# A mixer and 32 experts on one Trainium2 core: expert 0's first features gathered in quarters on a weight layout of its own, and chunk 7 loaded in four pieces

## What is computed

```
hn  = rmsnorm(x, norm_mix)
z   = gelu(hn @ w_in);  u, v = split(z)            # w_in 2048 x 4096
v   = layernorm(v);     sv = (w_s * causal) v + b_s   # in chunks of 128 tokens, 8 groups
h   = x + (u * sv) @ w_out                          # w_out 2048 x 2048
t   = rmsnorm(h, norm_ffn)
g   = softmax(t @ w_group + b_group); best group;  two best of its 8 experts, with weights
y   = sum over the two experts e of weight * ((silu(t @ w_gate[e]) * (t @ w_up[e])) @ w_down[e])
out = rmsnorm(h + y, norm_final)
```

## Time and profile before

| | |
|---|---|
| median of 3 runs | 1198.08 us (1197.81 to 1198.56) |
| the profiled execution | 1198.11 us, of it 1196.4 us span |
| busy: PE, PEld, DVE, ACT, POOL | 74%, 42%, 32%, 19%, 2% of the span |
| moved by DMA | 460.93 MB, 385 GB/s over the span |
| chain that ended last | DMA 50%, PE 47% |

### The profile page before, as it was taken

One profiled execution on the slowest core, in us unless ns is written; L12 is line 12 of the kernel. 1 busy time (PEld: TensorE's weight loads), 2 busy tenths in 40 slices (PEclk: granted clock), 3 DMA queues, 4 the chain that ended last, 5 costly groups with the idle time before them and its releaser, 6 DMA issues.

```text
span 1196.4 us, 17569 instructions
## 1 busy us (share of the span) xinstructions
PE 883.5 (74%) x7809; PEld 501.8 (42%) x7809; DVE 381.3 (32%) x493; ACT 231.6 (19%) x390; POOL 23.0 (2%) x66
## 2 busy tenths in 40 slices
PE   9999999999984666666666666666666666666666
PEld 7888888877431222222223232222222222222222
DVE  5454866545232222222222222222222222222233
ACT  6644655444200000000000000000000000000003
POOL 1200000000200000000000000000000000000000
PEclk9999999999997777778778787878787887878788
DMA  9875567878999999999999999999999999999997
GB/s 291 327 255 193 193 225 245 302 264 315 399 424 433 429 433 429 434 431 433 433 428 433 434 431 432 434 429 434 431 433 432 430 432 435 429 431 435 426 425 334
DMA packets 47686, 460.93 MB, mean 385 GB/s; under 512 B 4025, under 2 KB 4641, under 8 KB 32289
## 3 DMA queue, kind: packets, MB, share of 16 engines
q1 hardware_dynamic: 46704, 457.19, 92.4%
q0 software_dynamic: 864, 3.21, 0.8%
q10 hardware_dynamic: 80, 0.02, 0.0%
HBM read 458.05 MB, written 2.36 MB: 385 GB/s over the span
## 4 chain that ended last, share of the span: by engine, by line
DMA 50%; PE 47%; SPq 1%; ACT 1%; DVE 1%; issue 1%; POOLq 0%; DVEq 0%
DMA high_slots<-in_e_w_up 48%; PE scattered_out L1395 21%; PE bank L1605 12%; PE bank L1703 5%; PE pair L1566 3%; PE scattered_out L1716 1%; PE pair L1574 1%; DMA out_h<-acc 1%; ACT arena L780 1%; SPq L453 0%; DMA h<-in_x 0%; DVE acc L1261 0%; SPq L469 0%; PE pair L1582 0%; PE bank L1502 0%
## 5 line engine op out<-in xcount | busy, mean ns | idle before, releaser
L1199 DVE TENSOR_TENSOR acc<-scattered_out,acc 128x2048 f32<-128x2048 f32 x58 | 132.9, 2292 | 616.9 <-PE scattered_out L1716 616.9
L1605 PE MATMUL bank<-low_slots,arena 128*32 128x256 f32 x2048 | 153.5, 455 | 147.4 <-DMA low_slots<-in_e_w_up 147.0
L1605 PE MATMUL bank<-high_slots,arena 128*32 128x256 f32 x1952 | 146.0, 457 | 138.4 <-DMA high_slots<-in_e_w_up 138.4
L1605 PEld LDWEIGHTS bank<-low_slots,arena 128*32 128x32 f32 x2048 | 83.9, 126 | 218.8 <-issue 188.8
L1605 PEld LDWEIGHTS bank<-high_slots,arena 128*32 128x32 f32 x1952 | 79.6, 127 | 206.3 <-issue 178.7
L893 DVE TENSOR_TENSOR w_lo<-w_raw,w_hi 128x1024 fp32r<-128x1024 f32 x95 | 116.5, 1226 | 113.8 <-ACT w_hi L601 113.4
L601 ACT CAST w_hi<-w_raw 128x1024 fp32r<-128x1024 f32 x95 | 99.9, 1051 | 126.8 <-PE scattered_out L1395 120.7
L1395 PE MATMUL scattered_out<-w_hi,xT_second 128*128 128x512 f32 x376 | 121.4, 394 | 0.2 <-DVE w_lo L893 0.2
L1395 PE MATMUL scattered_out<-w_hi,xT_first 128*128 128x512 f32 x376 | 120.5, 393 | 0.1
L796 ACT COPY arena<-bank 128x256 f32<-128x256 f32 x32 | 11.9, 372 | 547.9 <-PE bank L1605 547.9
L1703 PE MATMUL bank<-down_slots,arena 128*32 128x512 f32 x944 | 107.9, 596 | 0.7 <-DVE arena L1193 0.7
(11 more groups left out here) (271 smaller groups left out, 512.1 us busy)
## 6 DMA issues: line engine op xcount, KB each, us to landing
down_slots<-in_e_w_down SPq DMA_DIRECT2D x26, 4096.0 KB, 21.1
low_slots<-in_e_w_gate SPq DMA_DIRECT2D x13, 4096.0 KB, 30.2
low_slots<-in_e_w_up SPq DMA_DIRECT2D x13, 4096.0 KB, 39.3
high_slots<-in_e_w_gate SPq DMA_DIRECT2D x13, 4096.0 KB, 30.5
high_slots<-in_e_w_up SPq DMA_DIRECT2D x13, 4096.0 KB, 39.7
w_raw<-in_a_w_in SPq DMA_DIRECT2D x64, 512.0 KB, 3.7
w_raw<-in_a_w_out SPq DMA_DIRECT2D x32, 512.0 KB, 5.0
down_slots<-in_e_w_down SPq DMA_DIRECT2D x6, 2048.0 KB, 19.4
```

Of the source, the lines that this page charges most:

```text
L1199: dve.tensor_tensor(acc[:, t, :], OUT[:, :], (acc if e else h)[:, t, :], ALU.add).then_inc(acc_done, 1)
L1605: ins = pe.matmul(GU[c * CAP:(c + 1) * CAP, 0:256], rows_k, gate_columns(rows_of[c // 2][k], c % 2), start=(a == 0 and k == 0), stop=(a == ...
```

## The change

Four things are changed.

1. Expert 0's gate and up weights (chunks 0 to 3) are loaded in another layout: partition p holds rows p, 128 + p, 256 + p and so on, eight separate rows of 2 KB instead of one piece of 16 KB. A gather for expert 0 now takes 128 neighbouring columns of `h`, and the gains come from `g_ffn`, which stands in that layout already.
2. Of the first eight steps' features, two quarters of 512 features are gathered, copied, transposed and scaled one after the other. The first quarter's four gate steps need only the first. VectorE's product for the first quarter and ScalarE's copy for it stand ahead of the sums and exponentials of the routing weights. The gather of the second half of the features stands behind gate steps 0 to 3 now, whole; before, one token tile of it stood ahead of gate step 0, and the other behind step 1.
3. Chunk 7 is loaded in four parts of 512 KB (rows c and c + 4, after `w_used` 89 + c).
4. The last half of the last block (half 7) goes into raw slot 0 instead of 3, so it waits for `lo_done` 93 instead of 92, and chunk 8's part over raw slot 3 is loaded first, after `lo_done` 92, the one over slot 0 last.

```diff
-        XE_FIRST, TRX_FIRST = GU[:, 256:512], TRX[:, 256:512]
+        XE_FIRST = (GU[:, 256:384], XE[:, 256:384])
+        TRX_FIRST = (TRX[:, 256:384], TRX[:, 384:512])
...
+        def raw_of(n, hc):
+            return 4 if n == 3 * NB - 1 and hc == HC - 1 else hc % 4
...
                 w, a = (e_gate, e_up)[c % 2], c // 2
+                if e == 0:
+                    return w[0, 0].rearrange("(k p) n -> p k n", p=P)[:, 8 * a:8 * a + 8, :]
                 return w[0, e].rearrange("(p a k) n -> a p k n", a=2, k=8)[a]
...
-                    sp.wait_ge(lo_done, HC * n + hc - 3)
-                sp.dma_start(w_raw[:, hc % 4, :, :], src).then_inc(raw_in[hc % 4], 16)
+                    sp.wait_ge(lo_done, HC * n + hc - 3 + raw_of(n, hc) // 4)
+                r = raw_of(n, hc) % 4
+                sp.dma_start(w_raw[:, r, :, :], src).then_inc(raw_in[r], 16)
...
-            sp.wait_ge(w_used, 3 * NB * HC - 6)
-            load_rows(7, 0, x_in[1])
-            sp.wait_ge(w_used, 3 * NB * HC - HC // 2)
-            load_rows(7, 1, chunk_in[chunk_at(7)[0]])
-            for q in range(4):
-                if q == 3:
-                    sp.wait_ge(w_used, 3 * NB * HC - 2)
-                    load_rows(9, 0, x_in[0])
-                sp.wait_ge(lo_done, 3 * NB * HC - 3 + q)
...
+            def load_pair(c, landed):
+                sp.wait_ge(w_used, 3 * NB * HC - 7 + c)
+                sp.dma_start(chunk_tile(7)[:, c:8:4, :], expert_chunk(7)[:, c:8:4, :]).then_inc(landed, 16)
+            def load_raw(q, count, landed):
+                sp.wait_ge(lo_done, count)
+                sp.dma_start(chunk_tile(8)[:, 2 * q:2 * q + 2, :], expert_chunk(8)[:, 2 * q:2 * q + 2, :]).then_inc(landed, 16)
+            load_pair(0, x_in[1])
+            load_pair(1, x_in[2])
+            load_raw(3, 3 * NB * HC - 4, raw_in[3])
+            load_pair(2, x_in[3])
+            load_half(w_out_half((NB - 1) * NBLK, HC - 1), 3 * NB - 1, HC - 1)
+            load_pair(3, chunk_in[chunk_at(7)[0]])
+            load_raw(1, 3 * NB * HC - 2, raw_in[1])
+            load_raw(2, 3 * NB * HC - 1, raw_in[2])
+            sp.wait_ge(w_used, 3 * NB * HC - 2)
+            load_rows(9, 0, x_in[0])
+            load_raw(0, 3 * NB * HC, chunk_in[chunk_at(8)[0]])
...
+            act.wait_ge(xe_first_ps, 1)
+            act.copy(xe[:, 0:P], XE_FIRST[0]).then_inc(xe_first, 1)
             for i in range(2):
                 act.wait_ge(exp_in, i + 1)
                 act.activation((g_exp, e21)[i], (g_shifted, d21)[i], ACT.Exp).then_inc(exp_done, 1)
+            act.wait_ge(xe_first_ps, 2)
+            act.copy(xe[:, P:2 * P], XE_FIRST[1]).then_inc(xe_first, 1)
...
+            dve.wait_ge(exp_in, 2)
+            dve.wait_ge(xeT_first_ps, 1)
+            scale_first(0, 1, TRX_FIRST[0], xeT_first)
             dve.wait_ge(exp_done, 2)
...
             def first_expert():
-                for t in range(NT):
-                    ins = gather_first(0, t)
-                ins.then_inc(xe_first_ps, 1)
+                gather_quarter(0, 0)
+                gather_quarter(0, 1).then_inc(xe_first_ps, 1)
+                gather_quarter(1, 0)
                 pe.wait_ge(xe_first, 1)
-                transpose_first(0).then_inc(xeT_first_ps, 1)
-                gather_first(1, 0)
+                transpose_quarter(0).then_inc(xeT_first_ps, 1)
+                gather_quarter(1, 1).then_inc(xe_first_ps, 1)
...
                 pe.wait_ge(xeT_first, 1)
                 gate_up_of(0, 0, rows_of, 0, 2).then_inc(gu_pair, 1)
-                gather_first(1, 1).then_inc(xe_ps, 1)
+                pe.wait_ge(xe_first, 2)
+                transpose_quarter(1).then_inc(xeT_first_ps, 1)
                 gate_up_of(0, 0, rows_of, 2, 4).then_inc(gu_pair, 1)
+                gather_second_half(0)
+                gather_second_half(1).then_inc(xe_ps, 1)
+                pe.wait_ge(xeT_first, 2)
                 gate_up_of(0, 0, rows_of, 4, 8).then_inc(gu_half, 1)
```

More of the change, by code:

```diff
@@ L393, in _ @@
             for n in range(NB):
-                for hc in range(HC):
+                for hc in range(HC if n < NB - 1 else HC - 1):
                     load_half(w_out_half(n * NBLK, hc), 2 * NB + n, hc)
@@ L599, in hi_half @@
                     act.wait_ge(w_used, HC * n + hc - 1)
-                act.wait_ge(raw_in[hc % 4], 16 * (2 * n + hc // 4 + 1))
-                act.copy(w_hi[:, hc % 2, :, :], w_raw[:, hc % 4, :, :]).then_inc(hi_done, 1)
+                r = raw_of(n, hc) % 4
+                act.wait_ge(raw_in[r], 16 * (2 * n + hc // 4 + 1 + raw_of(n, hc) // 4))
+                act.copy(w_hi[:, hc % 2, :, :], w_raw[:, r, :, :]).then_inc(hi_done, 1)
             def gelu_block(n, parity, dst, done):
@@ L1031, in _ @@
                 for hc in range(HC):
-                    lo_half(n, hc)
+                    lo_half(n, hc, raw_of(n, hc))
                     if hc == 1:
@@ L1175, in _ @@
             g_of = g_rows[:, :].rearrange("p (b k) -> p k b", k=KC).unsqueeze(3).to_broadcast([P, KC, NQ, CAP])
[L1177 to L1184, removed]
             def scale_xeT(e):
@@ L1583, in transpose_scat, with gather_quarter, gather_second_half, transpose_quarter @@
                 ins.then_inc(scat_ps, 1)
-            def gather_first(half, t):
+            def gather_quarter(q, t):
                 pe.wait_ge((sel_first, sel_ready)[t], 1)
                 for j in range(NB):
-                    cols = h[:, t, :].rearrange("q (p a j b) -> q a j p b", a=2, j=NB, b=2)[:, half, j, :, :]
-                    ins = pe.matmul((XE_FIRST, XE)[half][j * CAP:(j + 1) * CAP, 0:2 * P], sel[:, 0, t, :], cols,
+                    col = q * NBLK + j * P
+                    ins = pe.matmul(XE_FIRST[q][j * CAP:(j + 1) * CAP, :], sel[:, 0, t, :], h[:, t, col:col + P],
                                     start=(t == 0), stop=(t == NT - 1))
                 return ins
[L1594 to L1598, removed]
-                return ins
+            def gather_second_half(t):
+                for j in range(NB):
+                    cols = h[:, t, :].rearrange("q (a j p) -> q a j p", a=KC, j=NB)[:, 2:4, j, :]
+                    ins = pe.matmul(XE[j * CAP:(j + 1) * CAP, 0:2 * P].rearrange("c (a p) -> c a p", a=2), sel[:, 0, t, :],
+                                    cols, start=(t == 0), stop=(t == NT - 1))
+                return ins
+            def transpose_quarter(q):
+                return pe.transpose(TRX_FIRST[q], xe[:, q * P:(q + 1) * P], ident[:, :])
             def gate_up_of(e, a, rows_of, lo, hi):
                 for k in range(lo, hi):
-                    rows_k = xeT[:, 2 * a + k % 2, k // 2, :] if e == 0 else xeT[:, k % KC, 2 * a + k // KC, :]
+                    rows_k = xeT[:, 2 * a + k // KC, k % KC, :] if e == 0 else xeT[:, k % KC, 2 * a + k // KC, :]
                     for c in range(NQ):
@@ L1648, in wait_chunk @@
                 if i == 7:
-                    pe.wait_ge(x_in[1], 32)
+                    for c in range(3):
+                        pe.wait_ge(x_in[1 + c], 32)
                 if i == 9:
@@ L1652, in wait_chunk @@
                 if i == 8:
-                    for q in range(3):
-                        pe.wait_ge(raw_in[q], 16 * (3 * NB * HC // 4 + 1))
+                    for q in range(1, 4):
+                        pe.wait_ge(raw_in[q], 16 * (3 * NB * HC // 4 + (1, 1, 0)[q - 1]))
                 if i == 17:
```

24 lines of the change are left out of this document (14 added, 10 removed).

## The result

| | median | lowest to highest | runs |
|---|---|---|---|
| before | 1198.32 us | 1197.15 to 1199.95 | 22 |
| after | 1200.72 us | 1199.33 to 1202.17 | 22 |

The ratio is 1.0020, 95% interval 1.0014 to 1.0025: 2.4 us slower, where 1.2 us of gain was forecast. The profiled execution took 1201.8 us, 1.1 us above the median of its kernel, and its span is 1199.7 us (before 1196.4). So the traces differ by 3.3 us where the medians differ by 2.4.

A forecast was written before the change was run, and what follows sets the result against it. The prediction took TensorE's mixer to bound the kernel up to about 292 us and DMA bytes after; chunk 7, half 7 and the rows at 0 plus 0.70 and 0.50 from two holes gave 1.2 us gain: 1196.9 us, range 1196.0 to 1198.3.

The forecast's parts named there:

- What bounds the kernel: TensorE's mixer up to about 292 us; behind it the end is a sum of DMA bytes, at 431 GB/s from 333 us.
- Chunk 7 in four pieces: Mixer's end, 273 to 293 us: at most 2.5 us of queue time moved forward, all given back by 293; value 0.
- Half 7 later by a step: Last output block: issued at 278.2 instead of 275.44, landing 283.3 to 285.5, hidden until 286.2; cost 0, at most 1.7 us.
- Chunks 0 to 3 in rows of 2 KB: Expert 0's weight loads during the mixer: 0.5 us more for chunk 2, bounds 0 and 2.3, hidden by 1.1 us cover.
- The first features in quarters: Expert 0's first gates, about 298 to 308 us: `gu_pair` 1 earlier by 0.85 us, `gu_pair` 2 by 1.2, `gu_half` by 0.3.
- The sum: DMA holes at 303 to 305 and 306 to 308: 0.70 plus 0.50 gives 1.2 us gain, all reaching the end.
- the dry moment of 292: Queue falls to 229 GB/s in 292 to 294 us, awaiting the mixer's last matmul; only unused DMA time behind it counts.
- the holes stay: Rival for 303 to 308 us: small-transfer start-up or the later gates bind; gain only 0.3, time 1197.8 us; chance 25%.
- the hole of 303 to 305: Queue at 264 GB/s, 0.70 us unused, ended by `gu_pair` 1's issue at 302.14; forecast closed by an issue 0.85 us earlier.
- The chances: Whole kernel's time against before: within 0.2% 0.92, faster 0.05, slower 0.03; the forecast's own case 60%.
- small pieces pay their own start-up: Rival at the mixer's end: two more pieces expose 2.3 us each, 291.64 issue 2.6 us late, 1199.5 us; chance 5%.

The follow-up runs named there:

- e3: Kernel before with only the quarters of the first features, adapted to 16 KB rows (strided single-column gather): 1199.80 us, ratio 1.0013.
- e4: Changed kernel whole, but expert 0's chunks in the 16 KB rows of before and the quarters adapted to them: 1199.92 us, ratio 1.0011.
- e2: Kernel before with only the part on chunk 7, the late last half and the raw slots: 1197.95 us, ratio 0.9998.
- e1: Kernel before with only expert 0's four weight chunks read in 2 KB rows (features pair with wrong weight rows): 1200.16 us, ratio 1.0016.
- e6: Kernel before with 2 KB rows for chunks 0 and 1 alone: 1200.31 us, ratio 1.0018.
- e7: Kernel before with 2 KB rows for chunks 2 and 3 alone: 1198.29 us, ratio 0.9998.
- e8: Changed kernel with chunks 0 and 1 each issued as four 512 KB loads, one behind every second half, instead of one of 2 MB: 1198.82 us, ratio 1.0004.
- e11: Changed kernel with chunks 0 and 1 each in four 512 KB loads, issued one behind the other where the 2 MB load stood: 1198.55 us, ratio 1.0003.
- e13: Kernel before with the 2 KB rows and chunks 0 and 1 in pieces behind every second half, nothing else: 1199.24 us, ratio 1.0006.
- e14: The kernel of e12 run again, beside e13 on the same chip: 1199.00 us, ratio 1.0008.
- e9: e8 with the gather of the second half of the first features moved behind the gate matmuls of features 4 to 7: 1198.88 us, ratio 1.0006.
- e12: Changed kernel without the part on chunk 7, with chunks 0 and 1 in pieces behind every second half: 1199.14 us, ratio 1.0010.

## Why the prediction was wrong, point by point

- *What bounds the kernel.* Right. Behind M the remainder is 903.9 to 904.9 us in all kernels but e3 and e4, and a late mixer passes to the end: the kernels with the rows' stall are 1.8 to 2.4 us slower than before, those without it are between 0.3 us faster and 1.2 us slower.
- *Chunk 7 in four pieces.* Right at 0. The pieces fill the stretch from 26.6 to 11.6 us ahead of M, the 265 to 280 us of the earlier trace rows: 216 GB/s in the changed kernel and 221 in e2, where before has 184. It is given back: M to M+3 has 195 GB/s in e2 against 289 before. e2 is at 0.9998.
- *Half 7 later by a step.* Right, hidden. It is issued at 281.92, M-13.5, lands 7.2 us later, inside the bounds of 3.6 and 9.7, and its cast waits 2.16 us for it, half a microsecond more than for TensorE; the last dozen of matmuls starts straight behind the logits all the same. e2, where the cast waits 2.00 us, loses nothing.
- *Chunks 0 to 3 in rows of 2 KB.* **This step failed, and with it the sign.** "All four loads lie in the mixer, where the queue has room; chunk 2 is the one nearest to a wait": I looked for the place where a cast already waited for the queue, found only chunk 2, and priced its cover of 1.1 us. (Two more casts of the kernel before waited for the queue, at 216.92 and 239.90, behind chunks 5 and 6, which the change leaves alone.) At chunks 0 and 1 the releaser was TensorE, and I took that for room. It was not: the half behind chunk 0 is issued at 43.88 and took 8.3 us, so it landed at 52.2, 0.4 us ahead of the cast at 52.61; the one behind chunk 1 was issued at 66.78, took 8.0 and landed 0.7 ahead of the cast at 75.44. The price was also taken too low. I chose 0.5 us between bounds of 0 and 2.3; the loads of chunks 0 and 1 land 2.2 and 3.4 us later (9.3 to 11.5, 8.2 to 11.6), at the bound from the 291 GB/s of the first slice and past it. I had leaned on halves in 2 KB rows that land in 3.6 us, a load of 256 rows, where this one has 1024. At chunk 2, the only one that I worked through, the price was too high instead: it lands no later than before. e1, e6 and e7 show the cost at exactly these two chunks, e8 and e11 take nearly all of it away.
- *The first features in quarters.* The times came as worked out: `gu_pair` 1 0.88 us earlier (0.85 forecast), `gu_pair` 2 0.95 (1.2), `gu_half` 0.08 (0.3).
- *The sum.* **This step failed too**: "0.70 + 0.50 = 1.2 us, all behind the dry moment of 292 and ahead of the full stream, so all of it reaches the end". The rival "the holes stay" (25%) came nearest. Leaving e3 and e4 aside, the seven profiled executions without quarters move over M to M+25 between 378 and 387 GB/s, and the seven with them 376 to 392; the remainders from M average 904.3 and 904.4 us, where 1.2 us less was forecast; e13 and e14 agree. What the first two issues bring earlier is gone by the third, which is not earlier and so lets the queue thin out in front of it: the hole of 303 to 305 (M+11 to M+13, 277 GB/s) has 297 in the changed kernel, and between 260 and 328 in the others, with no order by the quarters. That a late `gu_half` costs (e3, e4) and an early one gives nothing (e9, whose next issue is later) fits: the earlier issues count only as far as the whole row of them moves. This last is argued from these kernels, not isolated.
- *The chances.* The side of the loss was mis-sized with it. No rival had the mixer lose time by the small rows, though I had priced the case at 1.2 us shown. The rival "small pieces pay their own start-up" gave the nearest time, 1199.5 us, but by another mechanism, the pieces of chunk 7, which e2 shows to cost nothing.

Left open: the kernels with pieces behind every second half (e8, e9, e12 to e14) lie 0.3 to 1.2 us above before, with a wait of 0.5 to 1.4 us for the queue at a cast near 43 us. Measured against the first casts, the casts behind that place are 0.2 to 1.1 us late in these kernels, and at M 0.5 us or less is left. So the pieces move a part of the stall to another half; whether that is all of it was not tried. None of the versions beats the kernel before.

## What to carry to other kernels

An engine that waits for another engine is no proof that the transfer had room: work out when the transfer landed against when it was needed, at every place that a load touches, and take the smallest cover. When a tile's layout turns a few long rows into many short ones, look at what is issued behind that load; cutting the load into several, or reading two neighbouring rows as one, took most of the cost away here. And an issue that comes earlier is worth only what the following issues let through.

## What was not expected of the hardware

- One load of 2 MB in 1024 rows of 2 KB (chunk 1 in e1) comes to 384 GB/s only between 6 and 8 us behind its issue, at a DMA share of 0.94 and more; in 128 rows of 16 KB the queue moves 421 GB/s from 2 to 8 us behind the issue, against 316. The same rows in four loads lose half as much (367). Chunks 0 and 3 show the same: from 2 to 4 us behind the issue the queue moves 459 and 425 GB/s before, 263 and 227 in e1. Chunk 2 does not: 327 before, 329 in e1, and it lands 10.7 us behind its issue in both. What is different there was not found, so this is no rule for every load. The Trainium skill (DMA: Bandwidth & Descriptors, Specifications) gives 512 bytes as the least transfer for full rate; at 2 KB this case is well above that and three of the four chunks still lose, so here the measurement decides.
- A matmul that reads f32 columns 64 bytes apart takes nearly twice as long with single columns (1.12 us for 16 of 128 columns against 0.65; 2.00 for 16 of 256 against 1.04) and hardly longer with pairs: the kernel before takes two neighbouring columns out of every 16 (`"q (p a j b) -> q a j p b"`, with `b=2`), 16 matmuls of 256 columns in 1.12 us. The Trainium skill (SBUF — State Buffer, Specifications (TRN2)) has lines of 16 bytes and asks for two hits in a line for full rate; the rows agree.
- A short pause of TensorE can cost as much again by the clock: in e6 the granted clock fell for 3.4 us behind a pause of 1.8 us (mean 0.55 in 82.70 to 86.40), at a price of some 1.9 us. Three other kernels with pauses of 1.5 to 1.7 us there kept 1.00. It was seen in one execution.
